# One step of a hybrid attention and convolution encoder on one core: squares a step behind in the out-projection, operands of the first FFN block in another order, token chunks of 256+256+256+288 and 248+280

## What is computed

```python
mix = jnp.concatenate([attn.reshape(B, S, D_ATTN), y_conv], axis=-1) @ w_out
x = x + g1 * mix                                        # g1, g2: gates, one per stream
h = rms_norm(x, norm_ffn_g) * (1 + sc2) + sh2
ff = (jax.nn.silu(h @ w_gate) * (h @ w_up)) @ w_down    # inner width 2816
x = x + g2 * ff
y = rms_norm(x, final_norm_g)
```

## Time and profile before

| | us |
|---|---|
| median of 3 runs | 1500.95 (1500.71 to 1502.23) |
| profiled execution | 1498.16 |
| its span, first to last instruction | 1496.4 |
| PE busy | 1422.0 (95%) |
| DVE busy | 880.1 (59%) |
| ACT busy | 433.7 (29%) |
| mean granted clock of PE | 0.962 of full |

### The profile page before, as it was taken

The page is one execution under the profiler, slowest core; times in us unless marked ns, Lnnn a source line. Parts: engine busy times, 40 slices in busy tenths (PEclk is TensorE's granted clock), DMA queues, the critical chain, the costliest instruction groups (busy, mean ns, idle before and its releaser), DMA issues.

```text
span 1496.4 us, 23691 instructions
## 1 busy us (share of the span) xinstructions
PE 1422.0 (95%) x9438; PEld 1294.4 (86%) x9438; DVE 880.1 (59%) x1440; ACT 433.7 (29%) x701; POOL 29.1 (2%) x33
## 2 busy tenths in 40 slices
PE   6899999999898899999769999999999999999987
PEld 6899999999664455558769999999999999999986
DVE  4888888342711325646785556555565655556556
ACT  4421110122101144342563232232313223231323
POOL 0000000000101011100000000000000000000000
PEclk8599999999998999999969999999999999999999
DMA  9344434310204012101001121111211011021202
GB/s 349 94 127 127 126 126 99 124 43 14 92 0 100 12 41 40 21 3 41 1 28 58 31 69 42 56 29 55 70 41 57 28 56 56 28 70 42 70 14 117
DMA packets 111518, 97.22 MB, mean 65 GB/s; under 512 B 9160, under 2 KB 96800, under 8 KB 111472
## 3 DMA queue, kind: packets, MB, share of 16 engines
q1 hardware_dynamic: 111264, 96.54, 21.5%
q10 hardware_dynamic: 208, 0.06, 0.0%
HBM read 84.57 MB, written 5.55 MB: 60 GB/s over the span
## 4 chain that ended last, share of the span: by engine, by line
PE 85%; DVE 9%; ACT 4%; issue 1%; DMA 0%; ACTq 0%; SPq 0%; DVEq 0%
PE PS L1001 30%; PE PS L672 18%; PE PS L1019 16%; PE PS L892 4%; PE PS L911 4%; PE PS L796 3%; PE PS L1101 1%; PE PS L832 1%; PE PS L870 1%; DVE ACC L1622 1%; PE PS L853 1%; PE PS L779 1%; PE PS L654 1%; ACT HH L1197 1%; ACT XJ L1175 1%
## 5 line engine op out<-in xcount | busy, mean ns | idle before, releaser
L1001 PE MATMUL PS<-HBH_T,EH 128*128 128x264 f32 x704 | 190.1, 289 | 15.4 <-DVE HBL_T L2000 7.8
L1967 DVE TENSOR_TENSOR EL<-HALF_W,EH 128x512 fp32r<-128x512 f32 x175 | 120.4, 688 | 135.3 <-ACT EH L1376 134.2
L1001 PE MATMUL PS<-HBL_T,EH 128*128 128x264 f32 x704 | 189.5, 289 | 0.0
L1376 ACT ACTIVATE EH<-HALF_W 128x512 fp32r<-128x512 f32 x175 | 109.7, 627 | 261.0 <-PE PS L1019 151.3
L672 PE MATMUL PS<-HH,WH 128*128 128x352 f32 x504 | 164.5, 327 | 7.2 <-DVE HL L1666 6.6
L2085 DVE SCALAR_TENSOR_TENSOR X<-PS,MOD,X 128x792 f32<-128x792 f32 (+2 forms) x240 | 125.3, 577 | 70.3 <-PE PS L1019 70.2
L672 PE MATMUL PS<-HL,WH 128*128 128x352 f32 x504 | 163.2, 324 | 0.0
L1019 PE MATMUL PS<-AL,EH 128*128 128x264 f32 x640 | 162.7, 285 | 0.0
L1019 PE MATMUL PS<-AH,EH 128*128 128x264 f32 x640 | 162.3, 284 | 0.0
L1001 PEld LDWEIGHTS PS<-HBH_T,EH 128*128 128x128 f32 x704 | 135.0, 192 | 16.8 <-issue 11.3
L1001 PE MATMUL PS<-HBH_B,EH 128*128 128x264 f32 x528 | 141.0, 287 | 6.0 <-DVE EL L1967 6.0
(11 more groups left out here) (256 smaller groups left out, 2503.9 us busy)
## 6 DMA issues: line engine op xcount, KB each, us to landing
ADA<-in_w_ada SPq DMA_DIRECT2D x16, 1024.0 KB, 5.3
HALF_W<-in_w_gate SPq DMA_DIRECT2D x22, 512.0 KB, 3.8
HALF_W<-in_w_up SPq DMA_DIRECT2D x22, 512.0 KB, 3.9
HALF_W<-in_w_down SPq DMA_DIRECT2D x22, 512.0 KB, 3.7
RAW<-in_w_in SPq DMA_DIRECT2D x20, 512.0 KB, 6.3
ADA<-in_w_ada SPq DMA_DIRECT2D x4, 2048.0 KB, 15.6
XR<-in_x_prompt SPq DMA_DIRECT2D x8, 512.0 KB, 4.5
out<-ORW SPq DMA_DIRECT2D x8, 512.0 KB, 2.8
```

Of the source, the lines that this page charges most:

```text
L1001: mm = pe.matmul(PS[:, 2 * s + n, 0:HQ], w, x[:, k, n * HQ:(n + 1) * HQ], start=(first and w is wh and x is xh), stop=(ends and w is wl), ...
L1376: act.activation(dst if len(src.shape) == 2 else dst.rearrange("p (k c) -> p k c", k=2), src, ACT.Copy)\
L1967: dve.tensor_tensor(el, src, eh.bitcast(F32), ALU.subtract).then_inc(entry_lo, 1)
```

## The change

Three parts.

1. Order in the out-projection. `finish_last_pair(1)` is split: its reciprocals stay, its scaling, rounding and rest come behind the second drain. `sum_square(t, m)` runs behind the drain of block m + 1 instead of that of block m. The rests of weight blocks 5 to 7 and the scalings and rests of the first half are dealt out anew.
2. Order of the first FFN group. The normalised blocks get buffers of their own (N11, N21, N12, N22), and the rests are written over their sources. So T4 must be made before the rest of T2, and DVE now makes T4 beside T2's rests and T3 after them; ACT rounds B22 without waiting for T4.
3. Chunks. All products whose drain multiplies by a gate take their tokens in chunks that keep the 1024 prompt tokens apart in equal runs: 256+256+256+288 for the loop's down products, 248+280 for the second half of the out-projection and of the last down products. The drain then has two instructions, one for the prompt (1024 or 496 columns) and one for the 32 stream tokens.

The load of the final gain `GF` moves behind the last weight loads.

```diff
+SQ = S // 4
+TAIL = (S - HT) // 2
+LATE = ((0, TAIL), (TAIL, HT - TAIL))
+QUARTERS = tuple((n * SQ, SQ + (SD if n == 3 else 0)) for n in range(4))
+def half_chunks(t):
+    return LATE if t else ((0, HQ), (HQ, HQ))
...
+        N11, N21, N12, N22, T1F = (at(name, [P, KH, HT], F32, half_part(n))
+                                   for n, name in enumerate(("N11", "N21", "N12", "N22", "T1F")))
...
-            sp.wait_ge(entry_lo, ENTRIES)
-            sp.dma_start(GF[:], final_norm_g[None, :].broadcast_to([P, D])).then_inc(gain_loaded, 16)
             for n in range(2):
                 load_half(4 + n, wd[:, 2 * (NG - 1):2 * NG, n * 512:(n + 1) * 512], 2, (7, 13)[n], NG - 1)
+            sp.wait_ge(product_full, PRODUCTS * (NG - 1) + 14)
+            sp.dma_start(GF[:], final_norm_g[None, :].broadcast_to([P, D])).then_inc(gain_loaded, 16)
...
-                        for n in range(4):
+                        for n, (q, width) in enumerate(QUARTERS):
                             for x in xs:
-                                mm = pe.matmul(PS[:, b + n, 0:HQ], w, x[:, k, n * HQ:(n + 1) * HQ],
+                                mm = pe.matmul(PS[:, b + n, 0:width], w, x[:, k, q:q + width],
...
-                if 2 <= m < 6:
-                    for q in range(2 * m - 4, 2 * m - 2):
-                        src = (NL[0], NHI)[q // KH][:, q % KH, 0:HT]
+                for q in ((), (0,), (1, 2), (3, 4), (5, 6), (7,), (), ())[m]:
+                    src = (N11, N21)[q // KH][:, q % KH, :]
...
-            act.wait_ge(operand_lo, 4 * KH)
-            act.wait_ge(t4_made, KH)
             for k in range(KH):
-                round_operand("B22", k, NHI[:, k, HT:T])
+                act.wait_ge(n2_full, KD + 2 * k + 2)
+                round_operand("B22", k, N22[:, k, :])
             act.wait_ge(product_full, 4)
             act.activation(part(SG, 0, 1), slot(0), ACT.Copy).then_inc(kept_act, 1)
-            act.wait_ge(operand_lo, 5 * KH)
             for k in range(KH):
-                round_operand("T4", k, NHI[:, k, 0:HT])
+                act.wait_ge(t4_made, k + 1)
+                round_operand("T4", k, N21[:, k, :])
...
-                    for src, c, st in ((PS[:, 2 * s, 0:HQ], slice(HT, HT + HQ), 0),
-                                       (PS[:, 2 * s + 1, 0:S - HT - HQ], slice(HT + HQ, S), 0),
-                                       (PS[:, 2 * s + 1, S - HT - HQ:HQ], slice(S, T), 1)):
-                        ins = dve.scalar_tensor_tensor(X[:, m, c], src, MOD[:, G1 + m, st:st + 1], X[:, m, c],
-                                                       ALU.mult, ALU.add)
+                    dst = X[:, m, HT:S].rearrange("p (n c) -> p n c", n=2)
+                    dve.scalar_tensor_tensor(dst, PS[:, 2 * s:2 * s + 2, 0:TAIL], MOD[:, G1 + m, 0:1], dst,
+                                             ALU.mult, ALU.add)
+                    dst = X[:, m, S:T]
+                    ins = dve.scalar_tensor_tensor(dst, PS[:, 2 * s + 1, TAIL:TAIL + SD], MOD[:, G1 + m, 1:2], dst,
+                                                   ALU.mult, ALU.add)
...
-            finish_last_pair(0)
+            invert_last_sums(0)
+            scale_last_output(0)
             rest_ao(4)
-            finish_last_pair(1)
+            invert_last_sums(1)
             for m in range(KD):
                 add_half(0, m)
-                if m >= 1:
-                    sum_square(0, m)
-                if m < 3:
-                    rest_ao(m + 5)
+                if m == 1:
+                    scale_last_output(1)
+                if m >= 2:
+                    sum_square(0, m - 1)
+                if 1 <= m < 4:
+                    rest_ao(m + 4)
+            sum_square(0, KD - 1)
...
             for m in range(KD):
                 add_half(1, m)
-                if m >= 1:
-                    sum_square(1, m)
+                if m >= 2:
+                    sum_square(1, m - 1)
...
-                for q in ((), (0, 1), (2, 3), (4, 5), (6,), (7,), (), ())[m]:
+                for q in ((), (0, 1), (2, 3), (4, 5), (6, 7), (), (), ())[m]:
                     scale_half(q, 0)
-                for q in ((), (), (0,), (1,), (2, 3), (4,), (5, 6), ())[m]:
+                for q in ((), (), (0,), (1, 2), (3, 4), (5, 6), (7,), ())[m]:
                     rest_first(q)
...
-            rest_first(7)
+            sum_square(1, KD - 1)
...
             for k in range(KH):
-                difference(NL[1][:, k, :], NHI[:, k, HT:T], NL[1][:, k, :], t3_made)
-                rest_operand("T2", k, NL[0][:, k, :], 13 + k)
+                dve.wait_ge(t2_made, k + 1)
+                difference(N21[:, k, :], N21[:, k, :], N11[:, k, :], t4_made)
+                rest_operand("T2", k, N11[:, k, :], 13 + k)
             rest_weights(4, "P7", 0, 0)
             for k in range(KH):
-                dve.wait_ge(t2_made, k + 1)
-                difference(NHI[:, k, 0:HT], NHI[:, k, 0:HT], NL[0][:, k, :], t4_made)
-                rest_operand("T3", k, NL[1][:, k, :], 17 + k)
+                difference(N12[:, k, :], N22[:, k, :], N12[:, k, :], t3_made)
+            for k in range(KH):
+                rest_operand("T3", k, N12[:, k, :], 17 + k)
```

More of the change, by code:

```diff
@@ L210, in build, with half_part @@
         SQ3 = at("SQ3", [P, 2, HT], F32, 8 * U + 24576)
[L211 to L214, removed]
-        SG = at("SG", [P, 2, T], F32, 8 * U + 24576)
[L216 to L222, removed]
+        SS3 = [at("SS3_0", [P, HT], F32, B + 65024), at("SS3_1", [P, HT], F32, B + 35584)]
+        def half_part(n):
+            return B + 1792 + 2 * n * U
+        AH = at("AH", [P, 2, T], F32R, half_part(14))
+        AL = at("AL", [P, 2, T], F32R, half_part(15))
+        UP = at("UP", [P, 2, T], F32, half_part(15))
+        SG = at("SG", [P, 2, T], F32, 8 * U + 24576)
+        N11, N21, N12, N22, T1F = (at(name, [P, KH, HT], F32, half_part(n))
+                                   for n, name in enumerate(("N11", "N21", "N12", "N22", "T1F")))
+        HBH = {name: at(f"HBH_{name}", [P, KH, HT], F32R, half_part(n))
+               for name, n in (("T1", 5), ("T2", 6), ("B22", 7), ("B11", 8), ("B21", 9), ("T3", 12), ("T4", 13))}
+        HBL = {name: at(f"HBL_{name}", [P, KH, HT], F32R, half_part(n))
+               for name, n in (("T2", 0), ("T4", 1), ("T3", 2), ("B22", 3), ("T1", 4), ("B11", 10), ("B21", 11))}
         HALF_W = at("HALF_W", [P, RING, KD * P], F32, 8 * U)
@@ L945, in ao_step @@
                 for w, xs in ((wh, (ao[0], ao[1])), (wl, (ao[0],))):
-                    for n in range(2):
+                    for n, (c, width) in enumerate(half_chunks(t)):
                         for x in xs:
-                            c = t * HT + n * HQ
-                            mm = pe.matmul(PS[:, 2 * ao_slot(g) + n, 0:HQ], w, x[k][:, c:c + HQ],
+                            c0 = t * HT + c
+                            mm = pe.matmul(PS[:, 2 * ao_slot(g) + n, 0:width], w, x[k][:, c0:c0 + width],
                                            start=(first and w is wh and x is ao[0]), stop=(last and w is wl))
@@ L1097, in last_down @@
                         for w, xs in ((eh[:, c:c + P], (AH, AL)), (el[:, c:c + P], (AH,))):
-                            for n in range(2):
+                            for n, (c0, width) in enumerate(half_chunks(t)):
                                 for x in xs:
-                                    q = t * HT + n * HQ
-                                    mm = pe.matmul(PS[:, 2 * s + n, 0:HQ], w, x[:, k, q:q + HQ],
+                                    q = t * HT + c0
+                                    mm = pe.matmul(PS[:, 2 * s + n, 0:width], w, x[:, k, q:q + width],
                                                    start=(k == 0 and x is AH and xs[-1] is AL),
@@ L1431, in _ @@
             for k in range(KH):
-                modulate(NL[1][:, k, :], k, 1)
-                modulate(NHI[:, k, HT:T], KH + k, 1)
+                modulate(N12[:, k, :], k, 1)
+                modulate(N22[:, k, :], KH + k, 1)
                 act.wait_ge(t1_made, k + 1)
@@ L1441, in _ @@
                 act.wait_ge(t2_made, k + 1)
[L1442 removed]
+                round_operand("T2", k, N11[:, k, :])
             round_weights(4, "P7", 0, 0, 0)
@@ L1908, in finish_last_pair, with scale_last_output @@
                 ins.then_inc(rcp_ready, 1)
+            def scale_last_output(t):
+                j = NJ - 1
                 c = slice(t * HT, (t + 1) * HT)
@@ L2078, in add_down @@
                 b = 4 * (1 - m % 2)
-                for src, t, st in ((PS[:, b:b + 3, 0:HQ], slice(0, 3 * HQ), 0),
-                                   (PS[:, b + 3, 0:S - 3 * HQ], slice(3 * HQ, S), 0),
-                                   (PS[:, b + 3, S - 3 * HQ:HQ], slice(S, T), 1)):
+                for src, t, st in ((PS[:, b:b + 4, 0:SQ], slice(0, S), 0),
+                                   (PS[:, b + 3, SQ:SQ + SD], slice(S, T), 1)):
                     dst = X[:, m, t]
```

(17 more changed lines are left out.)

25 lines of the change are left out of this document (12 added, 13 removed).

## The result

The changed kernel takes 1489.34 us (median of 4 runs, 1487.61 to 1490.23), the kernel before on the same chip 1500.94: a ratio of 0.992, 95% interval 0.9902 to 0.9937, 11.6 us less. Forecast was 1488.0 in 1484.0 to 1492.5. The profiled execution took 1489.81 us with a span of 1488.0, 8.4 under that of before.

A forecast was written before the change was run, and what follows sets the result against it. TensorE was taken to bound the FFN loop, VectorE the out-projection's second half; terms -6.5 - 4.1 - 1.0 - 0.9 - 0.4 = -12.9 us, giving 1485.3 in the profiled execution's terms, 1488.0 against the median, range 1484.0 to 1492.5.

The follow-up runs named there:

- u_scale: The changed kernel with the scaling of the first half's last output put back ahead of the out-projection's first drain; 1489.24 us, ratio 0.9926 to the kernel before.

## What to carry over

An instruction that waits for another engine inside a queue that is itself the bound costs that wait each time and for all that stands behind it: put a step of other work between the producer and the wait, and look for this before shortening any instruction (7.4 us against 0.5 here). Drains that uneven chunks make shorter pay only where the draining engine bounds: the loop paid 1.2 us on PE for time that DVE had to spare. Where PE waits a few microseconds ahead of a dense stretch on the path, matmuls that nobody reads in that wait kept its clock here, and cost nothing as long as they ended before the wait did. Where the next wait ends at a time that doesn't hang on the stretch made faster, they buy nothing: T2's product took 2.88 instead of 5.20 us, and set 2 came at 94.89 either way.

## What the runs showed of the hardware

- Behind equal idle gaps the clock sometimes fell and sometimes not: 2.20 us, then 0.69; 2.22 us, then 1.00; and 2.3 us, then a fall in the kernel before and none in u_scale. Behind filled gaps it stayed at 1.00 in all four kernels with filling before P1 and all three with filling in the tail. A price for the clock behind one gap is thus uncertain by 1.5 us, half a product, and a gain of 2 us upstream can vanish in it.
- This operand type shows no slower rate at 248 columns (113 ns from start to start on the mean of 94), and 256+256+256+288 columns cost 6 ns more per twelve matmuls than four times 264 each.
- The start of the out-projection scatters over 3.7 us from execution to execution with the same code ahead of it: compare stretches from a common instruction, not spans.
